# A forget-gate row and two silu gates, rewritten inside a three-stage transformer block

## The reference

```python
# block 1, Fox heads: softmax attention with forget gates, 8 heads of 64
log_f  = log_sigmoid(h @ w_forget + b_forget)            # 256 x 8
cum    = cumsum(log_f, axis=sequence)
logits = q.k / 8 + cum[query] - cum[key]
# block 1, retention heads: 4 heads of 128
ret = rms(retention(rq, rk, rv)) * ret_gain * silu(r_gate)
x   = x + gate * (concat(fox, ret) @ w_out)
# then an MLP, a second block (sparse attention, pooling, MLP), and a third:
o   = gla(q, k, v, loga)                                 # 4 heads of 256
o   = o * rsqrt(mean(o*o) + eps) * norm_g
x   = layer_norm(alpha*x + (o * silu(r)) @ c_w_out)
```

## Time and profile before

| | us |
|---|---|
| median of 3 runs | 1003.55 (1002.07 to 1003.96) |
| the profiled execution's own time | 1002.65 |
| its span in the profile | 1000.9 |
| TensorE busy | 964.9 (96%) |
| VectorE busy | 670.9 (67%) |
| ScalarE busy | 461.6 (46%) |
| GpSimd busy | 53.9 (5%) |

### The profile page before, as it was taken

The page is one execution under the profiler, slowest core; times in us unless marked ns, Lnnn a source line. Parts: engine busy times, 40 slices in busy tenths (PEclk is TensorE's granted clock), DMA queues, the critical chain, the costliest instruction groups (busy, mean ns, idle before and its releaser), DMA issues.

```text
span 1000.9 us, 13615 instructions
## 1 busy us (share of the span) xinstructions
PE 964.9 (96%) x4944; PEld 793.1 (79%) x4944; DVE 670.9 (67%) x867; ACT 461.6 (46%) x706; POOL 53.9 (5%) x59
## 2 busy tenths in 40 slices
PE   9899999799999999999899999999999999999996
PEld 7777877688888887977688888887776888888885
DVE  5877898795566576566876655677643876655657
ACT  5477545464454354544344544443652535544441
POOL 3040101100000001000020000001000010000000
PEclk9999999999999999899999999999999999999999
DMA  9988667596555676421375556565353446556541
GB/s 290 338 233 289 209 246 256 178 299 210 186 171 192 204 251 163 127 83 44 106 239 190 186 189 207 173 194 176 116 159 92 151 144 232 185 192 209 170 147 42
DMA packets 109987, 186.88 MB, mean 187 GB/s; under 512 B 8696, under 2 KB 67088, under 8 KB 109920
## 3 DMA queue, kind: packets, MB, share of 16 engines
q1 hardware_dynamic: 104800, 177.33, 54.4%
q0 software_dynamic: 2592, 8.53, 3.0%
q10 hardware_dynamic: 2544, 0.35, 0.2%
HBM read 185.13 MB, written 1.05 MB: 186 GB/s over the span
## 4 chain that ended last, share of the span: by engine, by line
PE 77%; DVE 10%; DMA 4%; ACT 4%; issue 3%; POOL 2%; SPq 0%; POOLq 0%; DVEq 0%; ACTq 0%
PE AT L1903 16%; PE PJ L1764 14%; PE PJ L1765 13%; PE PJ L1766 13%; PE AT L1905 8%; DVE wlo L1105 3%; DMA raw<-in_w_in_dram 2%; POOL rstd L477 2%; PE AT L1993 1%; ACT whi L591 1%; PE AT L1750 1%; DMA raw<-in_w_out_dram 1%; DMA raw<-in_w_ada_dram 1%; DVE acc L1131 1%; PE AT L2005 1%
## 5 line engine op out<-in xcount | busy, mean ns | idle before, releaser
L1903 PE MATMUL AT<-hT,whi 128*128 128x512 f32 x720 | 256.2, 398 | 0.0
L1105 DVE TENSOR_TENSOR wlo<-raw,whi 128x1024 fp32r<-128x1024 f32 x144 | 173.4, 1221 | 53.1 <-ACT whi L591 52.3
L1905 PE MATMUL AT<-hT,wlo 128*128 128x256 f32 x720 | 202.1, 281 | 0.0
L1231 DVE TENSOR_TENSOR wlo<-raw,whi 128x1024 fp32r<-128x1024 f32 x144 | 169.6, 1220 | 0.0
L591 ACT ACTIVATE whi<-raw 128x1024 fp32r<-128x1024 f32 x144 | 146.6, 1054 | 46.3 <-DMA raw<-in_w_in_dram 32.7
L1764 PE MATMUL PJ<-whi,uhi 128*128 128x512 f32 x408 | 160.8, 394 | 0.6 <-DVE ulo L1587 0.2
L1903 PEld LDWEIGHTS AT<-hT,whi 128*128 128x128 f32 x720 | 135.3, 188 | 32.9
L1765 PE MATMUL PJ<-wlo,uhi 128*128 128x512 f32 x408 | 159.2, 390 | 0.0
L1766 PE MATMUL PJ<-whi,ulo 128*128 128x512 f32 x408 | 158.9, 389 | 0.0
L1764 PE MATMUL PJ<-whi,hT 128*128 128x512 f32 (+1 forms) x344 | 141.7, 412 | 5.8 <-DVE hT L1288 1.9
L1241 DVE TENSOR_TENSOR pr<-AT,pr 128x512 f32<-128x512 f32 x45 | 31.1, 691 | 172.2 <-ACT pr L646 172.2
(11 more groups left out here) (313 smaller groups left out, 976.2 us busy)
## 6 DMA issues: line engine op xcount, KB each, us to landing
raw<-in_mlp_w_dram SPq DMA_DIRECT2D x128, 512.0 KB, 4.7
raw<-in_w_in_dram SPq DMA_DIRECT2D x32, 512.0 KB, 6.5
raw<-in_w_ada_dram SPq DMA_DIRECT2D x32, 512.0 KB, 5.5
raw<-in_w_mlp_in_dram SPq DMA_DIRECT2D x32, 512.0 KB, 4.8
raw<-in_w_mlp_out_dram SPq DMA_DIRECT2D x32, 512.0 KB, 4.7
raw<-in_c_w_in_dram SPq DMA_DIRECT2D x24, 512.0 KB, 4.5
raw<-in_w_ada_dram SPq DMA_DIRECT2D x32, 256.0 KB, 6.4
raw<-in_a_w_in_dram SPq DMA_DIRECT2D x12, 512.0 KB, 5.9
```

The costliest lines, as they stand in the source:

```text
L1105: tt(wlo[:, n % SPL, :], raw_slot(r), whi[:, n % SPL, :].bitcast(F32), ALU.subtract).then_inc(raw_done, 1)
L1231: tt(wlo[:, s % SPL, :], raw_slot(r), whi[:, s % SPL, :].bitcast(F32), ALU.subtract)\
L1903: mm(o, whi[:, s % SPL, c], hT[:, k, :, :].rearrange("p a s -> p (a s)"), start=k == 0, stop=False, skip_group_check=True)
L1905: ins = mm(o[:, 0:S], wlo[:, s % SPL, c], hT_hi[:, k, :], start=False, stop=k == KC - 1, skip_group_check=True)
```

## The change

Three things change, and no product on PE.

1. **Sums.** ACT copies the sums once each to `rows` (8 x 256, negated at partition 64, plain at 96). POOL then issues two transfers that read each row with a broadcast and write 8 x 2048 to `kT` and `qT`. PE waits for their landing (`ld_cum`). The two transfers stand in POOL's program ahead of the loads of rotary constants, gains and decay table, and `pool.wait_ge(cum_done, 2)` holds those back too.
2. **Block 1 gate.** ACT writes silu itself (function Silu in place of Sigmoid), frees the bank, and DVE's `ret_gates` is gone.
3. **Block 3 gate.** The same; `r_gain` multiplies the silu by the gain, and `gated` is gone.

```diff
+            pool.wait_ge(cum_done, 2)
+            for r, dst in ((64, kT), (96, qT)):
+                pool.dma_start(dst[r:r + 8, :].rearrange("r (h s) -> r h s", h=8),
+                               rows[r:r + 8, 1, 0:S].unsqueeze(1).broadcast_to([8, 8, S])).then_inc(ld_cum, 16)
             pool.wait_ge(mod_mm, 4)
             pool.dma_start(cst[:, C_MIX:], dram["const_c"][:, C_MIX:C_SBUF]).then_inc(ld_mix, 16)
...
+            def silu(z, e):
+
+                return nc.scalar.activation(e, z, ACT.Silu)
...
-            def minus_cum():
+            def cum_out():
 
                 act.wait_ge(cum_mm, 1)
-                act.wait_ge(acc_zero, 4)
-                nc.scalar.activation(kT[64:72, :].rearrange("r (h s) -> r h s", h=8),
-                                     AT[64:72, 1, 0:S].unsqueeze(1).broadcast_to([8, 8, S]), ACT.Copy,
-                                     scale=-1.0).then_inc(cum_done, 1)
+                nc.scalar.activation(rows[64:72, 1, 0:S], AT[64:72, 1, 0:S], ACT.Copy, scale=-1.0).then_inc(cum_done, 1)
+                nc.scalar.activation(rows[96:104, 1, 0:S], AT[96:104, 1, S:2 * S], ACT.Copy).then_inc(cum_done, 1)
...
                 for t in range(NT):
-                    gate(bank(7, t), proj[:, t, RG:RG + 512]).then_inc(gt_sig, 1)
+                    silu(bank(7, t), proj[:, t, RG:RG + 512]).then_inc(bank_free[1], 1)
...
-            def cum_rows():
-
-                dve.wait_ge(cum_mm, 1)
-                dve.wait_ge(ld_sel, 32)
-                nc.vector.tensor_copy(qT[96:104, :].rearrange("r (h s) -> r h s", h=8),
-                                      AT[96:104, 1, S:2 * S].unsqueeze(1).broadcast_to([8, 8, S])).then_inc(cum_done, 1)
...
-            def ret_gates():
-
-                for t in range(NT):
-                    o = proj[:, t, FK:FK + 512]
-                    dve.wait_ge(gt_sig, t + 1)
-                    tt(o, o, bank(7, t), ALU.mult).then_inc(bank_free[1], 1)
...
-                12: [cum_rows], 14: [lambda: maxima(0)], 15: [lambda: maxima(1)], 16: [lambda: maxima(2)],
+                14: [lambda: maxima(0)], 15: [lambda: maxima(1)], 16: [lambda: maxima(2)],
...
-                30: [ret_norm], 31: [ret_gates, ret_final],
+                30: [ret_norm], 31: [ret_final],
...
-            def gated(j, t):
-
-                dve.wait_ge(gt_sig, 2 + 2 * j + t + 1)
-                tt(out_at(j, t), out_at(j, t), r_at(j, t), ALU.mult).then_inc(src_ready, 1)
...
-                19: [lambda: r_gain(0), lambda: gla_var(0)], 20: [lambda: gla_var(1), gated_first],
+                19: [lambda: r_gain(0), lambda: gla_var(0)], 20: [lambda: gla_var(1), lambda: gla_norms(0)],
...
-                    pe.wait_ge(cum_done, 2)
+                    pe.wait_ge(ld_cum, 32)
```

More of the change, by code:

```diff
@@ L259, in block_program @@
         dseq, aseq = sem("dseq"), sem("aseq")
-        gt_sig = sem("gt_sig")
+        ld_cum = sem("ld_cum")
         ffT_mm, ffT_done, ff_mm, ff_abs, ff_ln, ff_done, cum_mm, cum_done = [sem(n) for n in (
@@ L624, in gate @@
                 return nc.scalar.activation(e, z, ACT.Sigmoid)
+            def silu(z, e):
+                return nc.scalar.activation(e, z, ACT.Silu)
             def gate_table():
-                gate(cst[:, C_ID:C_ID + 1], junk[:, :])
+                silu(cst[:, C_ID:C_ID + 1], junk[:, :])
             def mlp(m, s0):
@@ L845, in _ @@
                 11: [fox_gates],
-                12: [lambda: heads_out(0), lambda: heads_out(1), minus_cum],
+                12: [lambda: heads_out(0), lambda: heads_out(1), cum_out],
                 13: [lambda: heads_out(2), lambda: heads_out(3)],
@@ L1051, in r_gates @@
                 for t in range(NT):
-                    gate(bank(B_CIN + 4 + j, t), r_at(j, t)).then_inc(gt_sig, 1)
+                    silu(bank(B_CIN + 4 + j, t), r_at(j, t)).then_inc(bank_free[j], 1)
             tiles(T_CIN, T_COUT, {
@@ L1680, in _ @@
             r_at = lambda j, t: proj[:, t, 2048 + 512 * j:2048 + 512 * (j + 1)]
-            logit = lambda j, t: bank(B_CIN + 4 + j, t)
             out_at = lambda j, t: proj[:, t, half(j)]
@@ L1687, in r_gain @@
                 for t in range(NT):
-                    dve.wait_ge(gt_sig, 2 + 2 * j + t + 1)
[L1689 to L1692, removed]
+                    dve.wait_ge(bank_free[j], B_CIN + 4 + t + 1)
+                    ins = tt(out_at(j, t).rearrange("p (h d) -> p h d", h=2),
+                             r_at(j, t).rearrange("p (h d) -> p h d", h=2),
+                             acc[:, NG:NG + 256].unsqueeze(1).broadcast_to([P, 2, 256]), ALU.mult)
+                link(ins)
             def gla_norm(j, t):
@@ L1701, in gla_norm, with gla_norms @@
                     ins = stt(o, AT[:, 2 * t + j, c], rstd[:, k:k + 1], o, ALU.mult, ALU.mult)
-                return ins
-            def gated(j, t):
-                dve.wait_ge(gt_sig, 2 + 2 * j + t + 1)
-                tt(out_at(j, t), out_at(j, t), r_at(j, t), ALU.mult).then_inc(src_ready, 1)
-            def gated_first():
-                for t in range(NT):
[L1711 to L1717, removed]
+                ins.then_inc(src_ready, 1)
+            def gla_norms(j):
+                for t in range(NT):
+                    gla_norm(j, t)
             tiles(T_CIN, T_COUT, {
@@ L1721, in _ @@
                 16: [lambda: state(0)], 17: [lambda: state(1)], 18: [lambda: state(2)],
-                19: [lambda: r_gain(0), lambda: gla_var(0)], 20: [lambda: gla_var(1), gated_first],
+                19: [lambda: r_gain(0), lambda: gla_var(0)], 20: [lambda: gla_var(1), lambda: gla_norms(0)],
                 22: [lambda: quarter_lo(7, 0), lambda: quarter_lo(7, 1)],
-                23: [lambda: r_gain(1), norm_second, lambda: gated(1, 0), lambda: gated(1, 1)],
+                23: [lambda: r_gain(1), lambda: gla_norms(1)],
             })
```

## The result

The changed kernel takes 1010.47 us (median of 10 runs, 1005.45 to 1013.75), the kernel before 1002.66 (10 runs, 1000.34 to 1004.93). The ratio is 1.0064, with a 95% interval of 1.0046 to 1.0083: slower, where the prediction said 0.2% faster. The two medians alone are 7.8 us apart, which is 1.0078 and lies in the same interval.

The account below looks back on a forecast made before the run. It took TensorE to hold 77% of the chain, so only its waits counted: block 3 gate 0, block 1 gate -1.19, clock -0.47, sums -0.77, together -2.4 from 1003.55, giving 1001.2 us; range 999.8 to 1003.4.

Parts of the forecast that it names:

- the term of 0.75: At the scores, PE stalls 0.75 us because the second spreading transfer lands at 80.45, after 4.8 us, against 79.71 wanted.
- the 6.8: Upper bound for the second transfer's landing, from a 64 KB load under full weight stream; PE would stall 2.75 us.
- the selector's load: POOL's 64 KB load that took 6.8 us; transfers behaving like it would give 1003.1 us, chance 0.14.
- Rival D: Slower: the spreading transfers land late at the scores, past 82.9 us, each us costing PE one; 1005.3 or above, chance 0.07.
- -0.47: TensorE's clock behind the block 1 gate: with the 1.32 wait nearly gone, VectorE's 0.47 us wait for slow products comes back.
- The gain of 1.52 at `T_(0)` and `V_(0)`: PE's waits of 1.19 and 0.33 for ScalarE's last head copy and a copy of probabilities go, 1.52 us in all.
- the step given: With POOL's constant loads held back, ScalarE's weight tile lands at 80 rather than 83.24, so its last head copy ends earlier.
- Block 3 at 0: The block 3 gate gains 0, since PE is busy without a break from 745 to 798 us.
- Block 1, -1.19: In block 1's gate VectorE loses a 1.19 us multiplication ahead of a slot release, so the `w_out` tile lands 1.19 sooner.
- The stated row: Behind the block 1 gate, PE's wait of 1.32 us on the low part of `w_out` shrinks to about 0.1.
- fixed by the bytes in flight: Bound of the block 1 gate's gain: 0 if bytes in flight fix the `w_out` landing; as a rival 1002.8 us, chance 0.07.
- landings of 4.2 to 5.6 us: The spread of the spreading transfers' landing behind the main forecast, given as -1.6 to -2.9 us, chance 0.50.

Follow-up runs that it names:

- sums only: The kernel before with the forget-gate sums alone changed, both gates left as they were: 1010.16 us, ratio 1.0057.
- the stall filled: The changed kernel with 24 or 40 unread products on PE ahead of its wait for the transfers: 1004.07 us (ratio 1.0013) and 1005.72 us (1.0024).
- both repairs: The changed kernel with ScalarE's sum copies ahead of the head copies and POOL's four constant loads waiting for the first exponentials: 1002.09 us, ratio 0.9988.
- block 3 only: The kernel before with the silu pass in block 3's gate alone: 1003.35 us, ratio 0.9997.
- sums early: The changed kernel with ScalarE copying the sums ahead of the first head copies, so POOL issues before the weight loads: 1005.22 us, ratio 1.0004.
- gates, constants late: The kernel before with both silu gates, and POOL's four constant loads waiting for the first exponentials: 1001.19 us, ratio 0.9994.

## Why the prediction was wrong

**The landing of the spreading transfers (the term of 0.75).** This step failed. The prediction took 4.8 us, the mean of two gain loads, and gave the 6.8 as the upper bound; the second transfer took 9.8. It was wanted at 89.46 - 5.23 = 84.23 us, 4.65 after its issue at 79.58 (the prediction had 4.06), so 5.2 us of stall against 0.75. Most of the reason was there to be read. The gain loads of the earlier trace rows were issued at 72.1 and 72.7. SyncE's timeline of the kernel before shows when the stage's weight loads start:

```profile
73.81 0.34 SPq L371 DMA_DIRECT2D raw<-in_w_ada_dram  x1
74.94 0.37 SPq L371 DMA_DIRECT2D raw<-in_w_in_dram  x1
76.14 0.50 SPq L371 DMA_DIRECT2D raw<-in_w_ada_dram  x1
77.28 0.37 SPq L371 DMA_DIRECT2D raw<-in_w_in_dram  x1
80.92 0.34 SPq L371 DMA_DIRECT2D raw<-in_w_ada_dram  x1
```

The gain loads come before all of them; the transfers that the prediction put at 75.1 and 75.65 come behind two, of which its rows had the one at 74.94. It took the selector's load for one "issued in full flow, these before it"; in fact that load, issued at 58.49, had one weight load directly before it (57.50). The order of issue, the queues of other engines included, chose the row, not the nearness in time. An estimate from the table above: behind two weight loads the second transfer takes 8.0 to 8.3 us, so issued at 75.65 it lands at 83.7 to 84.0 and PE stalls 4.0 to 4.3 us, not 0.75. The other microsecond, to 5.2 in this execution, comes with the third weight load at 78.90: the kernel before has its third at the same distance from its first (76.14 after 73.81), but here the slow clock from 75 to 79 us had held the copies of the sums back until behind it. With sums only, the second transfer is issued just ahead of the third load, and the stall is 4.6. The change itself moves SyncE later: VectorE without its copy frees slots sooner, and weight loads follow at 81.23, 82.61 and 83.56, where the kernel before pauses from 77.28 to 80.92. The formula of the Trainium skill (DMA: Bandwidth & Descriptors, the anatomy of one DMA), from which the prediction worked out an estimate of 2.15 us for 64 KB, is met by no run here; 3.6 is the least.

**Rival D, priced at 0.07,** is the mechanism that came true: "the landing of `ld_cum`", deciding from a landing past 82.9, 7.2 us after the second issue. By its own arithmetic a landing after 9.8 us gives 9.8 - 4.06 - 3.2 = +2.5 us, and the rest moved by 2.0 to 2.8; the clock came on top. "For 64 KB at the head of its queue that is unlikely" was the error: it was at the head of its own queue, and still behind the others.

**TensorE's clock behind the new stall** was not in the sum at all, not even in D, which counted a us of PE for each us of lateness. The prediction used the clock only where a stall was to shrink (-0.47). Behind the stall the clock was 0.57 from 88 to 96 us; the products up to `T_(0)` took 2.8 us longer, and with the stall filled they did not; over whole runs the mean clock loss rose by 3.0 to 3.7 us, of which the part outside this stretch is not explained. The rule of the Trainium skill that the prediction cites (TensorE: Matmul & The Clock Gate, the HAM clock gate), a clock halved by default and released by recent activity, agrees in kind with the 0.57 behind 5.23 us of idleness; it should have been applied to the new stall and not to the old ones alone.

**The gain of 1.52 at `T_(0)` and `V_(0)`** came, but not by the step given. The tile did not land sooner: issued at 77.70, used at 86.43, 8.7 us, ScalarE's idle 4.11. The waits went because PE itself came 5 us later. Where POOL's constants are truly out of the way, the mechanism works (6.3 us, idle 2.60). The further weight loads are not what held the tile here: with both repairs they follow as closely, and the tile is used after 6.6 us. What differs is that POOL issues its six transfers between 78.92 and 81.88, while the tile is under way; that this is the cause was not tested by itself.

**The gates.** Block 3 at 0 was right. Block 1, -1.19 and -0.47 for the clock: measured -1.6 for it alone and -2.8 and -1.4 for both, so the size was right within the spread, the way there less so. The stated row came partly: PE's wait behind the gate was 1.3, 2.1 (sums only) and 0.9 us (block 3 only) in the three kernels without this edit, 1.4 on the mean, and from 0.2 to 1.3 in the eleven with it, 0.55 on the mean: 0.9 shorter, not 1.19. The last `w_out` tile took 9.2 to 10.3 us in the eleven, 8.7 to 9.9 in the three, 9.5 against 9.2 on the mean, so a part of the earlier issue may be lost in the landing, between the bounds "all of it" and "fixed by the bytes in flight". The term of the clock did not come in the changed kernel: in the 4 us from the first transposition of the MLP's input (187.04 before, 196.79 after) the granted clock was 0.59 and is 0.65, with the wait of 1.32 down to 0.3. It was 0.57 to 0.59 in the three kernels without the edit, 0.57 to 0.65 in seven of the eleven with it, and 1.00 in four; and where it was 1.00, the two waits of 2.2 grew to 5.0 or 5.1 in total, from 4.5.

**The sum, mended:** rest +5.2 (stall) - 1.5 (`T_(0)`, `V_(0)`) - 1.0 (behind the gate, 1.3 to 0.3 in these two profiles) = +2.7, measured +2.0 to +2.8; clock +3.0 to +3.7. Measured together 5.7 us, and 0.64% of 1003.55 is 6.4. One slip in the prediction's own sum changes nothing: landings of 4.2 to 5.6 us give -3.0 to -1.6, not -2.9 to -1.6.

## What to carry to other kernels

A copy on an engine that ends just in time is replaced by a transfer only with a landing taken from a transfer issued at the same place behind the other queues: count what all engines have issued and not yet landed. Here the second transfer of 64 KB took 4 us ahead of the weight stream and 8 to 10 behind two or three loads of 512 KB. A stall of TensorE can cost more than its length, here 5.2 us and 2.8 more for slow products behind it, and products that nobody reads, about as long as the stall, took some 5 us off. A silu in one pass gave nothing in block 3, where TensorE never waited, and perhaps 0.2% in block 1, where its second multiplication held back a slot release.

## What the hardware showed that was not expected

- The first packet of a transfer came 0.9 to 1.4 us after its issue with no weight load just before (sums early), but 4.1 to 4.6 us on POOL's queue behind three (changed kernel) and 5.0 to 5.4 us on ScalarE's (issued at 76.55), although the engines were busy only 0.47 from 76.5 to 78 us there. How the 16 engines share the queues was not settled.
- The effect runs both ways: with POOL's transfers issued first, a 512 KB weight tile took 10.45 us (sums early), and 6.3 at most with POOL silent (gates, constants late).
- Most of the run-to-run spread is the clock: the loss varied from 9.0 to 19.1 us in 28 runs of one kernel, with a standard deviation of 2.2, against 1.5 for the rest. Splitting each run's time this way told a fall of the rest by 1.3 and 2.2 us where the ratios told nothing, but it counts a slow clock during a stall as loss.
